# An MoE stage on one Trainium2 core: lists of 128 places, small operations ahead of the weight splits, and down projections in f32

## What is computed

```python
g_sel = jnp.argmax(g_logits, axis=-1)                   # one of 4 groups
top_v, top_i = lax.top_k(e_in, MOE_TOPK)                # 2 of its 4 experts
top_w = jax.nn.softmax(top_v, axis=-1) * g_w
...
for e in range(N_EXPERTS):                              # 16
    h = jax.nn.silu(xt @ w_g[e]) * (xt @ w_u[e])        # 1024 -> 512
    out = out + gates[:, e:e + 1] * (h @ w_d[e])        # 512 -> 1024
```

## Time and profile before

| | us |
|---|---|
| median of 3 runs (range) | 965.25 (963.96 to 967.22) |
| profiled execution | 968.07 |
| its span, first to last instruction | 966.3 |
| PE busy | 881.2 (91%) |
| DVE busy | 657.6 (68%) |
| ACT busy | 481.5 (50%) |
| moved by DMA | 178.06 MB, mean 184 GB/s |

### The profile page before, as it was taken

One profiled execution on the slowest core, in us unless ns is written; L12 is line 12 of the kernel. 1 busy time (PEld: TensorE's weight loads), 2 busy tenths in 40 slices (PEclk: granted clock), 3 DMA queues, 4 the chain that ended last, 5 costly groups with the idle time before them and its releaser, 6 DMA issues.

```text
span 966.3 us, 19139 instructions
## 1 busy us (share of the span) xinstructions
PE 881.2 (91%) x8164; PEld 591.7 (61%) x8164; DVE 657.6 (68%) x877; ACT 481.5 (50%) x681; POOL 85.6 (9%) x89
## 2 busy tenths in 40 slices
PE   6999999999999998999999979947999989889783
PEld 4434784855756655444444439937887768677661
DVE  5677769641887766643443444453899999988887
ACT  5434373223554445233223223562587878787842
POOL 7000000003000000000000000000122332112100
PEclk9989999999999999999999999965899999989887
DMA  8702404526631112943433406373899999999852
GB/s 212 178 24 54 121 25 109 154 66 188 171 96 34 29 32 61 373 117 108 120 92 89 125 23 223 129 290 104 300 364 386 398 394 392 381 393 386 328 215 89
DMA packets 122543, 178.06 MB, mean 184 GB/s; under 512 B 13357, under 2 KB 98661, under 8 KB 114262
## 3 DMA queue, kind: packets, MB, share of 16 engines
q1 hardware_dynamic: 116272, 162.76, 49.3%
q0 software_dynamic: 5904, 13.48, 5.1%
q10 hardware_dynamic: 278, 0.56, 0.2%
HBM read 170.54 MB, written 14.39 MB: 191 GB/s over the span
## 4 chain that ended last, share of the span: by engine, by line
PE 64%; DVE 16%; DMA 9%; ACT 7%; issue 3%; ACTq 0%; DVEq 0%; POOLq 0%
PE bank L977 17%; PE bank L978 16%; PE bank L979 16%; DVE arena L1732 8%; ACT arena L850 4%; PE bank L1190 3%; DMA arena<-in_moe_wd 3%; DMA arena<-in_moe_wu 3%; DMA arena<-in_moe_wg 3%; PE bank L1209 3%; PE bank L1084 1%; PE bank L1199 1%; PE bank L1307 1%; DVE arena L1838 1%; DVE arena L1848 1%
## 5 line engine op out<-in xcount | busy, mean ns | idle before, releaser
L977 PE MATMUL bank<-arena 128*128 128x96 f16 (+3 forms) x2336 | 511.0, 264 | 35.8 <-DVE arena L1838 26.3
L978 PE MATMUL bank<-arena 128*128 128x96 f16 (+3 forms) x2336 | 510.3, 264 | 0.0
L979 PE MATMUL bank<-arena 128*128 128x96 f16 (+3 forms) x2336 | 509.3, 264 | 0.5 <-issue 0.5
L977 PEld LDWEIGHTS bank<-arena 128*128 128x128 f16 (+1 forms) x2336 | 238.5, 102 | 137.8 <-issue 33.4
L979 PEld LDWEIGHTS bank<-arena 128*128 128x128 f16 (+1 forms) x2336 | 237.8, 102 | 78.2 <-issue 3.1
L978 PEld LDWEIGHTS bank<-arena 128*128 128x128 f16 (+1 forms) x2336 | 237.6, 102 | 68.5 <-issue 2.1
L1732 DVE SCALAR_TENSOR_TENSOR arena<-arena 128x2048 f16<-128x2048 f32 x96 | 216.9, 2287 | 39.1 <-ACT arena L850 38.9
L850 ACT ACTIVATE arena<-arena 128x2048 f16<-128x2048 f32 x96 | 180.8, 1905 | 13.7 <-DMA arena<-in_moe_wg 7.4
L617 ACT ACTIVATE arena<-arena 128x1024 f16<-128x1024 f32 (+1 forms) x92 | 92.5, 1007 | 102.5 <-PE bank L979 79.7
L1477 DVE SCALAR_TENSOR_TENSOR arena<-arena 128x1024 f16<-128x1024 f32 (+1 forms) x91 | 103.5, 1163 | 11.7 <-ACT arena L617 10.1
L671 ACT ACTIVATE arena<-bank 128x512 f32<-128x512 f32 x35 | 20.8, 595 | 92.0 <-PE bank L979 91.9
(11 more groups left out here) (273 smaller groups left out, 734.4 us busy)
## 6 DMA issues: line engine op xcount, KB each, us to landing
arena<-in_moe_wg SPq DMA_DIRECT2D x32, 1024.0 KB, 18.6
arena<-in_moe_wu SPq DMA_DIRECT2D x32, 1024.0 KB, 16.9
arena<-in_moe_wd SPq DMA_DIRECT2D x32, 1024.0 KB, 18.8
arena<-in_w_gate SPq DMA_DIRECT2D x32, 512.0 KB, 4.1
arena<-in_w_in SPq DMA_DIRECT2D x31, 512.0 KB, 4.0
arena<-in_w_branch SPq DMA_DIRECT2D x32, 192.0 KB, 3.6
y_rows<-in_c_tab SPq DMA_DIRECT2D x4, 1024.0 KB, 12.4
arena<-in_w_out SPq DMA_DIRECT2D x8, 512.0 KB, 5.3
```

The costliest lines, as they stand in the source:

```text
L977: pe.matmul(outb, lhs[0], rhs[0], start=first, stop=False, skip_group_check=True)
L978: pe.matmul(outb, lhs[0], rhs[1], start=False, stop=False, skip_group_check=True)
L979: return pe.matmul(outb, lhs[1], rhs[0], start=False, stop=last_, skip_group_check=True)
```

## The change

1. **Down halves whole.** `WHOLE` marks the d steps. They are not split: PE waits for the landing of the load itself and multiplies f32 `hid` by the f32 half, four matmuls of 512 columns for each half in place of 24. `split`, the split buffers and their counts run over the other 64 steps (`CUT`). The cut of `hid` (L928, L1843) is gone, and `hid` has two buffers. The slot of a d step is free only when PE has multiplied it (`slot_free`: `chunk_used` in place of `split_done`).
2. **Lists of 128 places.** The one-hot rows have 128 places (P) in place of 96, in the operations that make them and as the weights of L1297 and L1307. `CAP` stays 96 for all else.
3. **Tables ahead of the branch.** The one-hot rows are made before the branch; they lie elsewhere now. The rest of `told` is made in `tell_lists()` at step 1, the lists are multiplied after step 3 and read out in step 4.
4. **Small work first.** In each step, tanh, cuts, `hid` and copies out stand ahead of the split, and LOOK is 5. The split of step 5 moves from ahead of the branch into it. The load of the last gain (`load_nf`) moves to step 48.
5. **WARM.** Twelve matmuls of 512 columns, whose result nothing reads, stand ahead of the first transposes.
6. **Slots.** Steps 16, 17 and 18 load into slots 5, 6 and 7, which the splits of steps 5, 6 and 7 free; step 19 has the slot that waits for the lists. Step 20 uses slot 8, which step 8, the first d step, has to leave.

```diff
-LOOK = 4
+LOOK = 5
+WARM = 12
...
+WHOLE = [kind == "d" for kind, e, _ in STEPS]
+CUT = [c for c in range(len(STEPS)) if not WHOLE[c]]
...
-    numbers = np.repeat(np.arange(CAP, dtype=np.float16), NE)[None, :]
+    numbers = np.repeat(np.arange(P, dtype=np.float16), NE)[None, :]
...
-        SLOT = [*range(READY), *range(FIRST), READY, FIRST, READY + 1]
+        SLOT = [*range(READY), *range(FIRST), READY, *range(FIRST, READY - 2), READY + 1]
...
-        def splits_ahead(c):
-
-            return max((i + 1 for i in range(c) if SLOT[i] == SLOT[c]), default=0)
+        def slot_free(c):
+
+            last = max((i for i in range(c) if SLOT[i] == SLOT[c]), default=None)
+            if last is None:
+                return None
+            return ("chunk_used", last + 1) if WHOLE[last] else ("split_done", CUT.index(last) + 1)
...
-        onehot = view(XS, NT, CAP * NE // 2).bitcast(F16)
-        onehot_near = view(39436, NT, CAP * NEAR // 2).bitcast(F16).rearrange("p t (c e) -> p t c e", e=NEAR)
-        slots = view(19456, CAP * NE // 2).bitcast(F16)
+        onehot = view(9216, NT, P * NE // 2).bitcast(F16)
+        onehot_near = view(39436, NT, P * NEAR // 2).bitcast(F16).rearrange("p t (c e) -> p t c e", e=NEAR)
...
+        sgr, hid = view(XS + 768, KH * CAP), [view(a, KH * CAP) for a in (XS + 1152, 19456)]
...
-                    if splits_ahead(c):
-                        sp_.wait_ge(S("split_done"), splits_ahead(c))
-                    elif c > READY + FIRST:
+                    if slot_free(c):
+                        sp_.wait_ge(S(slot_free(c)[0]), slot_free(c)[1])
+                    elif c == READY + FIRST:
                         sp_.wait_ge(S("x2_stored"), 16 * NT)
+                    else:
                         sp_.wait_ge(S("token_full"), 2)
                     stage_load(c)
...
-            act.wait_ge(S("hgT_used"), KD)
-            for c in range(FIRST, NW):
-                split(c)
...
                 x_hi(0)
-                load_nf(nf)
+                act.wait_ge(S("hgT_used"), KD)
                 for c, (kind, e, hf) in enumerate(STEPS):
-                    if NW <= c + LOOK < len(STEPS):
-                        split(c + LOOK)
                     if kind == "g" and hf:
...
-                    if STEPS[c - 1][0] == "u" and STEPS[c - 1][2]:
-                        eh = STEPS[c - 1][1]
-                        act.wait_ge(S("h_ready"), eh + 1)
-                        if eh >= 2:
-                            act.wait_ge(S("chunk_used"), steps_to("d", eh - 2))
-                        act.activation(hgT[eh % 2][0], hid, ACT.Copy).then_inc(S("hhi_done"), 1)
                     if kind == "u" and hf and e + 1 < NE:
                         x_hi(e + 1)
...
+                    if c + LOOK in CUT[FIRST:]:
+                        split(c + LOOK)
+                    if c == len(STEPS) // 2:
+                        load_nf(nf)
...
-                    pe.wait_ge(S("onehot_ready"), 1 + NT)
+                    pe.wait_ge(S("onehot_ready"), 2 + NT)
                     for e in range(NE):
                         for t in range(NT):
-                            last = pe.matmul(ps[4][0:CAP, 5 * e:5 * e + 5], onehot[:, t, :].rearrange("p (c e) -> p e c", e=NE)[:, e, :],
+                            last = pe.matmul(ps[4][:, 5 * e:5 * e + 5], onehot[:, t, :].rearrange("p (c e) -> p e c", e=NE)[:, e, :],
                                              told[:, t, :, e], start=(t == 0), stop=(t == NT - 1))
...
+                for _ in range(WARM):
+                    pe.matmul(ps[2][:, :], w_hi[0][:, 0:P], w_hi[0][:, 0:512], start=True, stop=True)
                 x_transposes(0)
                 for c, (kind, e, hf) in enumerate(STEPS):
                     if kind == "d" and not hf:
-                        pe.wait_ge(S("hlo_done"), e + 1)
+                        pe.wait_ge(S("h_ready"), e + 1)
...
-                    pe.wait_ge(S("split_done"), c + 1)
-                    if kind == "d":
-                        v = [w[c % NW].rearrange("p (k n) -> p k n", k=2) for w in (w_hi, w_lo)]
-                        hi, lo = (h.rearrange("p (k c) -> p k c", c=CAP) for h in hgT[e % 2])
+                    if WHOLE[c]:
+                        pe.wait_ge(S(f"stage_landed{SLOT[c]}"), landed(c))
+                        v = stage[c].rearrange("p (k n) -> p k n", k=2)
+                        h = hid[e % 2].rearrange("p (k c) -> p k c", c=CAP)
                         for k in range(2):
                             for j in range(2):
-                                cs = slice(512 * j, 512 * (j + 1))
-                                last = products(y_bank(e)[j][0:CAP, :], (hi[:, 2 * hf + k, :], lo[:, 2 * hf + k, :]),
-                                                (v[0][:, k, cs], v[1][:, k, cs]), hf == 0 and k == 0, hf == 1 and k == 1)
-                    else:
-                        v = [w[c % NW].rearrange("p (k n) -> p k n", k=4) for w in (w_hi, w_lo)]
-                        hi, lo = xgT
-                        bank = ps[2 * (e % 2) + (kind == "u")]
-                        for k in range(4):
-                            for m in range(KH):
-                                last = products(bank[:, m * CAP:(m + 1) * CAP], [w[:, k, m * P:(m + 1) * P] for w in v],
-                                                (hi[:, 4 * hf + k, :], lo[:, 4 * hf + k, :]),
-                                                hf == 0 and k == 0 and m == 0, hf == 1 and k == 3)
+                                last = pe.matmul(y_bank(e)[j][0:CAP, :], h[:, 2 * hf + k, :], v[:, k, 512 * j:512 * (j + 1)],
+                                                 start=hf == 0 and k == 0, stop=hf == 1 and k == 1, skip_group_check=True)
+                        last.then_inc(S("chunk_used"), 1)
+                        continue
+                    i = CUT.index(c)
+                    pe.wait_ge(S("split_done"), i + 1)
...
-                    if c == 1:
-                        all_tokens()
                     if kind == "u" and hf and e + 1 < NE:
                         x_transposes(e + 1)
+                    if c == 3:
+                        all_tokens()
...
-            for c in range(FIRST, NW):
-                split(c)
+            dve.wait_ge(S("x2_ready"), NT)
+            for t in range(NT):
+                tell("onehot_ready", tt(*onehot_views(t), ALU.is_equal))
...
-                def h_lo(e):
-                    dve.wait_ge(S("hhi_done"), e + 1)
-                    tell("hlo_done", tt(hgT[e % 2][1], hid, hgT[e % 2][0], ALU.subtract))
...
+                def tell_lists():
+                    link(dve.tensor_copy(told[:, :, 2, :], selj[:, 1, :, :]))
+                    for j, w in enumerate((w1, w2)):
+                        link(tt(selj[:, j, :, :], selj[:, j, :, :], w.to_broadcast([P, NT, NE]), ALU.mult))
+                    link(tt(gates[:, :, :], selj[:, 0, :, :], selj[:, 1, :, :], ALU.add))
+                    link(ts(gates[:, :, :], gates[:, :, :], W16, None, ALU.mult))
+                    link(dve.tensor_copy(told[:, :, 3, :], gates[:, :, :]))
+                    tell("onehot_ready", tt(told[:, :, 4, :], gates[:, :, :], told[:, :, 3, :], ALU.subtract))
...
                 x_lo(0)
-                link(dve.tensor_copy(told[:, :, 2, :], selj[:, 1, :, :]))
-                for j, w in enumerate((w1, w2)):
-                    link(tt(selj[:, j, :, :], selj[:, j, :, :], w.to_broadcast([P, NT, NE]), ALU.mult))
-                link(tt(gates[:, :, :], selj[:, 0, :, :], selj[:, 1, :, :], ALU.add))
-                link(ts(gates[:, :, :], gates[:, :, :], W16, None, ALU.mult))
-                link(dve.tensor_copy(told[:, :, 3, :], gates[:, :, :]))
-                link(tt(told[:, :, 4, :], gates[:, :, :], told[:, :, 3, :], ALU.subtract))
-                dve.wait_ge(S("x2_stored"), 16 * NT)
-                for t in range(NT):
-                    tell("onehot_ready", tt(*onehot_views(t), ALU.is_equal))
                 for c, (kind, e, hf) in enumerate(STEPS):
-                    if c == 2:
+                    if c == 4:
                         all_slots()
-                    if NW <= c + LOOK < len(STEPS):
-                        split(c + LOOK)
-                    if STEPS[c - 1][0] == "u" and STEPS[c - 1][2]:
-                        h_lo(STEPS[c - 1][1])
-                    if c == 4 * NE // 2:
-                        dve.wait_ge(S("gain2_landed"), 48)
-                        for i in range(LAST):
-                            tell("onehot_ready", ts(onehot_T[i][0:CAP, :], tok_iota[0:CAP, :], slotv[0:CAP, 1, ROUTED + i:ROUTED + i + 1], None, ALU.is_equal))
-                    if kind == "d" and hf and e >= ROUTED:
-                        y_lo(e)
                     if kind == "u" and hf:
                         if e + 1 < NE:
...
+                        if e >= 2:
+                            dve.wait_ge(S("chunk_used"), steps_to("d", e - 2))
```

(7 more changed lines are left out.)

66 lines of the change are left out of this document (42 added, 24 removed).

## The result

| | before | after |
|---|---|---|
| median of 20 runs, us | 965.41 | 968.23 |
| ratio to before, 95% interval | | 1.0028 (1.0015 to 1.0040) |
| profiled execution, its span, us | 968.07, 966.3 | 967.75, 965.9 |

The forecast was 953.2 with a range of 944 to 964. The time is outside, 15 us above, and on the other side of before. In the profile of after the router is done 2.4 us earlier than in that of before (the CAST of the first tokens at 648.41 for 650.76), so times of after are compared with forecast times after adding 2.4.

What follows compares the result with a forecast made beforehand. It took DVE, then DMA, to bound the kernel, and DMA after the change. Last load 922.0, output rows 925.0, DVE's 13.2 to 938.2, unchanged 16.1: span 954.3, 12.0 less, median 953.2, range 944 to 964.

Steps and rivals of the forecast that it cites:

- PE's expert of 16.04 us: PE's work per expert with f32 down halves: 4 x 2.04 + 1.00 + 6.88 = 16.04 us, in place of 14.3.
- The lists at 5.3 us: The 64 list matmuls on PE after step 3: 0.083 us each, 5.3 us, bounds 1.8 and 15.3.
- rival B: The longer lists pay by column, 15.3 us for 5.3; median 963.2, the same as before; chance 0.15.
- Step 20's load at 692.5: Start of the stage: this load waits for step 8 on PE and goes out at 692.5, 3.3 us later than before.
- The hole: Gap in the load stream: DMA moved nothing from 670 to 675; after the change it idles from 680 to 692.
- 3.00 us for the mean load: DMA's price for a half of 1.0486 MB with the row traffic between: 3.00 us, 18.0 us an expert.
- The stream's end: End of the weight loads: 76 loads of 3.00 us after 692.5, plus 1.5, put the last load at 922.0.
- PE's own chain: PE from step 10 at 696.0 to 926.4, with the tail 947.7; 6.6 us shorter, so DMA decides.
- The gain is in this tail: Behind the last load no splits and no late `add_rows` are left; the span falls by 12.0 us.
- DVE bounds the first half of the stage, DMA the second: Kernel before: DVE at 16.03 us an expert uses up the loaded slots, then the chain waits 25.21 us for a load.
- rival E: Other losses, as stalls of ACT behind a late load that hold tanh and cuts; slower, chance 0.02.
- D: Rival: PE becomes the bound because weights of an f32 pass are not hidden; median 979, chance 0.07.

Runs made afterwards that it cites:

- e_nowarm: The changed kernel without the twelve matmuls meant to warm PE's clock; 968.27 us, ratio 1.0021 to the kernel before.
- e_spread: The changed kernel with list places renumbered so that filled and empty places spread over all positions; 957.82 us, ratio 0.9905 to the kernel before.
- e_f16o: The changed kernel with down halves split into f16 again and the queue order of before; 957.58 us, ratio 0.9890 to the kernel before.
- e_end: The changed kernel with the splits of steps 89 to 91 queued behind the cut of expert 15's tokens; 962.05 us, ratio 0.9954 to the kernel before.
- e_norows: The changed kernel without token gathers and expert row stores in the expert stage, output not the reference's; 952.78 us, ratio 0.9871 to the kernel before.

## Why the prediction was wrong, point by point

**Right.** The matmul of 512 f32 columns in two passes of 0.43: the 16 passes of two halves take 7.03 us. (A down half had 12 f16 matmuls before, three for each of four products, and not the 24 that the text ahead of the prediction says; 24 in two halves at 0.216 are the 5.18 us of the earlier trace rows.) PE's expert of 16.04 us: 16.03 in all runs without waits. The lists at 5.3 us: 4.1, 0.064 us a matmul for 0.179 before; rival B is out. The rule of the Trainium skill (TensorE: Matmul & The Clock Gate, Weight-path perf modes) gave an estimate of 7.6; the direction agrees, the gain here is larger. The one-hot rows are covered. WARM gives nothing: step 0 has matmuls 0.08 us apart until 662.1, at a granted clock of 0.50, and e_nowarm confirms it. Step 20's load at 692.5: 691.6. The hole "is not closed, it is moved": so it is. 3.00 us for the mean load: the same bytes were moved from 690 to 830 us.

**The stream's end, off by 7.6 us.** "Last load: 692.5 + 76 x 3.00 + 1.5 = 922.0" prices bytes over the mean of 16 engines. Eight of the 16 records of step 95's load are there at 915.8, 918.2 in the forecast's times; the last comes at 927.2, 929.6. The share of 1.02 in the earlier trace rows is a mean over engines and could not show that. What could have been asked is how far the records of one load lie apart. The 25 us from issue to landing alone would not have told: step 88's load takes 26.6 us in after and 25.9 in e_spread.

**PE's own chain, off by 21 us. This is the step that failed.** "PE's own chain: step 10 at 696.0 [...] to 926.4 [...] It is 6.6 us shorter, so DMA decides" let PE run beside the loads without a wait and compared only the ends. Each gate and up half must land and be split first, and behind the last of these PE has 22 to 24 us of work. PE ran without a pause until 805, 1 us ahead of the forecast, then it followed the last landings, through splits and the cuts behind them: 11 us were lost by the end of d13. A further 0.7 us are a wait at 910, 7.4 the wait for the cut of expert 15, and 1.7 the half clock after it (granted clock 0.50 from 921.5 to 924).

**"The gain is in this tail [...] no splits and no late `add_rows` are left."** Splits behind the last load did not bound before: e_f16o, which has them, is 10 us faster than before. In the tail f32 halves added 2.4 us of PE work. The sign of this term was wrong. (In the changed order f16 halves are 8 us slower, but by 17.8 us an expert all along and not by the tail.) What the change does win, 1.1%, is the start, which the prediction priced (step 4 8 us sooner) but let be lost in the hole. The hole belongs to the f32 halves: with f16 halves there is none (a DMA share of 1.02 from 680 to 690), and the gain stays.

**"DVE bounds the first half of the stage, DMA the second."** With rows spread DVE bounds all of it in before, at 16.03 us an expert, and PE bounds nearly all of it after the change, at 16.04. The change put one bound in place of an equal one. The prediction had both numbers and held neither against the other, since it took DMA's 18.0 for the price of the steady state.

**Rivals.** The cause that rival E named, ACT held behind a late load with the small work after it, was given 0.02 and cost some 7 us at expert 15 alone (e_end). D was right that PE can decide, with the wrong mechanism: weights of an f32 pass are hidden (7.03 us for 16 passes of 0.43). None of the rivals had an uneven load of the DMA engines, which cost 1.2% of either kernel.

## What to carry to other kernels

A load is done when its last part has landed, and the mean DMA share does not show how late that is. Where gathers or scatters with empty places run beside large loads, deal the filled places out over the positions before anything else is tuned; here it was worth 1.2% on two kernels for three lines. When an engine is relieved, hold the new bound against the old number by number (16.04 for 16.03), and follow each consumer behind the last input that it needs, with the work that stands behind it; comparing the ends of two streams is not enough. On an in-order engine, nothing that the critical engine waits for should stand behind an operation that waits for a load.

## What was not expected of the hardware

Indirect DMAs of 96 rows, of which on average the last 32 are empty, load the 16 DMA engines unevenly, as far as e_spread and e_norows show it: the parts of one 1 MB load drift apart from 1.6 us (step 24 of before) to 18 us (step 88), while the mean busy share reads 1.02. That positions go to engines in groups of six fits the five early records and the result of e_spread, but no run shows the mapping itself.

Matmuls of 5 columns whose weights are 128 columns that lie 16 elements apart start every 0.064 us (after), with 96 such columns every 0.179 (before). More columns take a third of the time.
